# Chunk 0 of a streaming encoder: four engines' queues written in another order

## The chip, the cores and the metric

The kernel runs on one core of one Trainium2 chip. A core has a matrix engine (TensorE, PE in the profile), a vector engine (VectorE, DVE), an activation engine (ScalarE, ACT), a general engine (GpSimd, POOL) and a queue that starts transfers (SyncE, SP). Each executes its own list strictly in order, and they meet only at semaphores. The metric is the device time of one execution in microseconds. Before the change it was 1473.51 us (median of 3 runs, 1473.25 to 1474.21).

## The reference, cut to what matters

One inference step of a one-layer encoder on 4096 prompt rows of 1024 channels, and on 64 sample rows.

```
h = rmsnorm(x) * norm_g
u = h @ w_in                  # 1024 x 2816: eleven splits of 256 columns
a_b, a_c, a_x, a_g, b_v, b_a, b_g, c_u, c_g, x_q, x_g = split(u)
y_a = a_b * conv3(a_c * a_x) * silu(a_g)
y_b = silu(layernorm(conv31(b_v * sigmoid(b_a)))) * silu(b_g)
y_c = (pool_linear(trailing_means(c_u) - c_u)) * pool_scale * silu(c_g)
y_x = softmax(x_q @ mem_k) @ mem_v * silu(x_g)
x = x + concat(y_a, y_b, y_c, y_x) @ w_out ;  y = rmsnorm(x) * final_norm_g
```

`mem_k`, `mem_v` of the prompt are projections of a normed memory of 256 rows. The outputs also hold the convolution and pooling states and the memory keys and values.

## The kernel before, in words

The prompt is worked in 16 chunks of N = 256 rows, and each chunk in two convolution channel tiles (CT = 2). Chunk 0 is written out apart (`first_chunk` on each engine), chunks 1 to 14 are a loop, and chunk 15 is written out with the sample. Chunk 0 does, beside a chunk's own work, all that is done once:

- **The input weights are split into two half precision parts.** 22 tiles of 1024 x 128 arrive by DMA. For tile j ACT squares it (`w_square(j)`, line 1123), PE sums the squares over partitions (`weight_sums(g)`, lines 640 and 642, one for two tiles), DVE makes a power of two from the sum (`w_scale(g)`, lines 1570 to 1575), ACT writes the high part (`w_high(j)`, line 1130) and DVE the low part (`w_low(j)`, line 1584). A projection of PE (`project`, lines 621 to 623, 48 matmuls of 256 columns) takes tiles 2g and 2g+1 of its split; the splits are in the order b_a, b_v, x_q, c_u, a_c, a_x, a_b, a_g, b_g, c_g, x_g, so b_g takes tiles 16 and 17, c_g 18 and 19, x_g 20 and 21.
- **The output weights are split into 16 pieces and stored.** SP loads piece p (`load_piece`, line 405), ACT writes its high part (`piece_hi`, line 1116), POOL its low part (`piece_lo`, line 2097), SP stores both parts (`keep`, line 409). The staging buffer has 4 slots, the ring 8.
- **The prompt memory** is projected in eight `memory_product` steps (line 875), and keys and values are split.
- **The sample** is normed, transposed on PE (`sample_transposes`, line 693), split by ACT (`sample_hi`) and DVE (`sample_lo`), and its eleven projections of 64 columns (`sample_project(g)`, lines 621 to 623 with `hs`, 48 matmuls each) fill PSUM banks that ACT copies out (`raw_keep(0)` after groups 0 to 3, `raw_keep(1)` after 4 to 7, line 1081).

The convolution of width 31 is 31 steps of two instructions on DVE (`taps(0, N, k0, k1)` does steps k0 to k1 - 1, line 1603). The attention is done for two pairs of heads: `scores(p)` on PE, `softmax_max(p)` and `softmax_rcp(p)` on DVE, `exps(p)` (line 1159) and `probs_hi(p)` (line 1173) on ACT, `probs_lo(p)` on DVE (lines 1630 and 360), then a transposition through memory on SP (`probs_leave(p)`, line 473, and `probs_arrive(p)`, line 477), then `attend(p)` on PE (line 730).

Three banks of PSUM (`U`) take the projections of chunk 0 in turn. The list `FIRST` says in which order, and `emptied` makes an entry wait until the entry three places before it has been read (`EMPTIED`): `b_g` waits for the third place before it, and so on. The bank of `a_b` is free when DVE has done `ab_out` (line 1726), that of `w9` when DVE has done `w_scale(9)`.

```
if type(i) is int and i == 0:
    n = FIRST.index(name) - 3
...
"a_b": (conv_a, 4 * CT), "a_g": (ag_ok, 1),
"mix": (mix_ok, 1), "b_g": (bg_ok, 1), "zf": (zt_ok, 1), "c_g": (cg_ok, 1),
```

After the projections PE runs the 16 output pieces (`out_pieces`), with `attend(0, N, 1)`, three sample groups and the transposes of z between them. Then chunk 1 begins.

Of the kernel before, what the change touches and what calls it, by code (L numbers as in the profile page):

```python
# [35 lines left out]
N = 256  # L36
# [20 lines left out]


FIRST = ["w0", "w1", "w2", "b_a", "b_v", "w3", "x_q", "w4", "w5", "w6", "c_u", "w7", "w8", "a_c", "a_x",
         "w9", "a_b", "a_g", "b_g", "w10", "c_g", "mix", "x_g", "zf", "zb", "r0", "r1", "r2", "r3"]  # L60


SAMPLE_SLOTS = {"mix": (1, 2), "zf": (2, 0), "zb": (3, 0)}
# [6 lines left out]
RAW, RING = 4, 8  # L70
Y_ORDER = [0, 4, 6, 2]
PIECES = 2 * KT
# [22 lines left out]
def encoder_program(nc, x_prompt, x_sample, mem_prompt, state_conv_a, state_conv_b, state_pool,  # L95
# [5 lines left out]
    with ctx:  # L101
# [292 lines left out]
        def _(sp):  # L394
# [50 lines left out]
            sp.wait_ge(kv_ok.sem, 2)  # L445
            for dst, off in ((new_k, 0), (new_v, GW)):
                sp.dma_start(dst[0, 0].rearrange("(t p) h d -> p t (h d)", p=P), kv[:, :, off:off + GW]).then_inc(kv_in.sem, 16)
            for p in range(RAW, PIECES):
                keep(p - RAW)
                load_piece(p)  # L450


            def store_states(k, outs):
                sp.wait_ge(st_ok.sem, 2 * k + 2)
# [31 lines left out]
            def probs_leave(i, p, n):  # L486
                sp.wait_ge(p_t_ok.sem, p_t_ok.at(i, p + 1))
                last = type(i) is int and i == CHUNKS
                put_out(probs_turned[PAIRS if last else p], work(i).turned_p, min(n, P), probs_out[p])
# [21 lines left out]
                sp.dma_start(ring[:, q % RING].bitcast(F32), wo_split[q]).then_inc(wo_in[q % RING].sem, 16)  # L511

            def first_sync(x_here, y_here, x_next, x_after):
                probs_leave(0, 0, N)
                for p in range(PIECES - RAW, PIECES):
                    keep(p)
                probs_arrive(0, 0, N)
                raw_leaves(0)
                probs_across(0, 1, N)
                sp.dma_start(xp, x_next).then_inc(x_in[1].sem, 16)  # L520
                raw_leaves(1)
                sp.wait_ge(wlo_ok.sem, FT)
# [96 lines left out]
        def _(pe):  # L619
# [259 lines left out]
            def first_chunk():  # L879
                pe.wait_ge(ident_ok.sem, 2)  # L880
                transposes(0, ob[:, 0])
                pe.wait_ge(tiny_ok.sem, 1)
                weight_sums(0)
                transposes(1, ob[:, 1])
                constants()
                weight_sums(1)
                weight_sums(2)
                project(0, N, "b_a")
                project(0, N, "b_v")
                memory_transposes(0, ob[:, 0])  # L890
                memory_transposes(1, ob[:, 1])
                weight_sums(3)
                project(0, N, "x_q")
                memory_product(0)
                weight_sums(4)
                for k in range(1, 4):
                    memory_product(k)
                weight_sums(5)
                memory_product(4)
                weight_sums(6)  # L900
                sample_transposes()
                memory_product(5)
                project(0, N, "c_u")
                memory_product(6)
                weight_sums(7)
                weight_sums(8)
                memory_product(7)
                project(0, N, "a_c")
                keys_t(0)
                value_sum(0)  # L910
                project(0, N, "a_x")
                scores(0, N, 0)
                weight_sums(9)
                project(0, N, "a_b")
                project(0, N, "a_g")
                scores(0, N, 1)
                for g in range(4):
                    sample_project(g)
                project(0, N, "b_g")
                weight_sums(10)  # L920
                for g in range(4, 7):
                    sample_project(g)
                project(0, N, "c_g")
                sample_project(7)
                attend(0, N, 0)
                mix(0, N)
# [12 lines left out]
                out_pieces(0, N, PIECES - 2 * CT, PIECES)  # L939
# [95 lines left out]
        def _(act):  # L1035
# [230 lines left out]
            def first_chunk(nxt):  # L1266
# [40 lines left out]
                for k in range(16, 18):  # L1307
                    w_square(k)
                w_high(11)
                sample_hi()  # L1310
                w_square(18)
                cu_out(0, N)
                w_high(12)
                keys_values()
                w_high(13)
# [7 lines left out]
                piece_hi(1)  # L1323
                scaled_out(0, N, "a_c", gate[:, 1, :, 0:N], ACT.Copy, ac_ok)
                w_high(15)
                for k in range(2, 5):
                    piece_hi(k)
                w_high(16)
                piece_hi(5)
                exps(0, N, 0)  # L1330
                for k in range(6, 8):
                    piece_hi(k)
                w_high(17)
                piece_hi(8)
                w_high(18)
                piece_hi(9)
                w_square(20)
                piece_hi(10)
                w_square(21)
                piece_hi(11)  # L1340
                d_high(0, N)
                probs_hi(0, N, 0)
                piece_hi(12)
                w_high(19)
                for k in range(13, 15):
                    piece_hi(k)
                act.wait_ge(wsq_ok.sem, FT)
                scaled_out(0, N, "a_g", gate[:, 2, :, 0:N], ACT.Silu, ag_ok)
                piece_hi(15)
                raw_keep(0)  # L1350
                exps(0, N, 1)
                for k in range(20, 22):
                    w_high(k)
                probs_hi(0, N, 1)
                b_gate(0, N)
                mixed(0, N)
                y_high(0, N, 0, ya[:, :, 0:N], ya_ok)
                c_gate(0, N)
# [102 lines left out]
        def _(dve):  # L1461
# [316 lines left out]
            def first_chunk(nxt):  # L1778
# [38 lines left out]
                sample_rms()  # L1817
                sample_scale()
                taps(0, N, 10, 11)
                pool_weights_lo()  # L1820
                taps(0, N, 11, 13)
                for k in range(9, 11):
                    w_low(k)
                taps(0, N, 13, 14)
                w_scale(6)
                taps(0, N, 14, 15)
                w_low(11)
                sample_lo()
                taps(0, N, 15, 16)
                w_scale(7)  # L1830
                w_low(12)
                taps(0, N, 16, 18)
                for k in range(13, 15):
                    w_low(k)
                taps(0, N, 18, 19)
                taps(0, N, 19, 20)
                keys_lo(0)
                w_scale(8)
                value_scale(0)
                taps(0, N, 20, 21)  # L1840
                values_lo(0)
                va_out(0, N)
                softmax_max(0, N, 0)
                w_low(15)
                taps(0, N, 21, 22)
                pool_diff(0, N)
                w_low(16)
                w_scale(9)
                softmax_rcp(0, N, 0)
                conv_a_taps(0, N)  # L1850
                taps(0, N, 22, 23)
                w_low(17)
                ab_out(0, N)
                probs_lo(0, N, 0)
                softmax_max(0, N, 1)
                w_low(18)
                taps(0, N, 23, 24)
                w_low(19)
                taps(0, N, 24, 25)
                ya_out(0, N)  # L1860
                d_low(0, N)
                w_scale(10)
                softmax_rcp(0, N, 1)
                for k in range(20, 22):
                    w_low(k)
                probs_lo(0, N, 1)
                taps(0, N, 25, 31)
                yx_out(0, N)
                z_stats(0, N)
                z_norm(0, N)  # L1870
# [331 lines left out]
```

## Time and profile before

| | |
|---|---|
| median of 3 runs | 1473.51 us |
| the profiled execution | 1474.04 us, of it the span of instructions 1472.2 us |
| PE busy | 1430.6 us (97% of the span) |
| DVE busy | 1180.9 us (80%) |
| ACT busy | 561.3 us (38%) |
| POOL busy | 216.5 us (15%) |
| mean granted TensorE clock | 0.996 of full |
| stretch of chunk 0 on PE | 0 to 166.1 us |

The times of the profile are those of the profiled execution, 0.5 us above the median of the runs. A matmul's busy time is modelled and overlaps its neighbours, so the distance between two starts is the better measure of what it costs.

### The profile page before, as it was taken

How to read it: one execution, taken by the hardware profiler on the slowest of the kernel's cores; microseconds unless marked ns; L12 is line 12 of the kernel's file. 1: busy time of each engine (PE TensorE's matmuls, PEld its weight loads, DVE VectorE, ACT ScalarE, POOL GpSimd, SP SyncE). 2: the span in 40 equal slices, each digit the busy share in tenths (PEclk: the TensorE clock that was granted, in tenths of full speed). 3: DMA queues.
4: the chain of work that ended last, by engine and by line, in shares of the span. 5: the costliest groups of instructions: out<-in, count | busy, mean ns of one | idle time of the engine just before them, and what ended most of it. 6: DMA issues, size and time to landing. Idle time of an engine off the chain costs nothing.

```text
span 1472.2 us, 32643 instructions
## 1 busy us (share of the span) xinstructions
PE 1430.6 (97%) x11766; PEld 1224.2 (83%) x11766; DVE 1180.9 (80%) x3087; ACT 561.3 (38%) x1237; POOL 216.5 (15%) x180
## 2 busy tenths in 40 slices
PE   5898999999999999999999999999999999999997
PEld 4687888888888888888888888888888888888875
DVE  6896696987959697895959789695968869596897
ACT  7775243333324333332434233243423423242342
POOL 0062011111101111110111111011111111111111
PEclk9999999999999999999999999999999999999999
DMA  9976455555364556446355654635565463545663
GB/s 265 259 268 211 170 174 188 200 199 199 114 239 146 185 199 227 172 128 252 118 197 188 228 185 139 251 107 203 182 215 187 160 247 91 216 168 199 231 206 118
DMA packets 127522, 280.88 MB, mean 191 GB/s; under 512 B 12297, under 2 KB 69309, under 8 KB 127485
## 3 DMA queue, kind: packets, MB, share of 16 engines
q1 hardware_dynamic: 127485, 280.40, 55.3%
q8 instruction: 22, 0.36, 0.1%
q14 instruction: 15, 0.12, 0.0%
HBM read 221.86 MB, written 58.49 MB: 190 GB/s over the span
## 4 chain that ended last, share of the span: by engine, by line
PE 87%; DVE 6%; DMA 2%; issue 2%; ACT 2%; SPq 2%; POOL 0%; ACTq 0%; DVEq 0%
PE u L621 20%; PE u L622 19%; PE u L623 19%; PE sps L621 5%; PE sps L623 4%; PE sps L622 4%; PE qps L621 4%; PE qps L623 4%; PE qps L622 4%; PE ops L730 2%; DVE z L1603 1%; DMA ring<-wo_split 1%; DMA w_hl<-in_w_in 1%; DVE w_hl L1584 1%; SPq L397 1%
## 5 line engine op out<-in xcount | busy, mean ns | idle before, releaser
L621 PE MATMUL u<-h_hi,w_hl 128*128 128x256 f16 x2816 | 770.1, 273 | 2.8 <-DVE w_hl L1584 2.7
L622 PE MATMUL u<-h_lo,w_hl 128*128 128x256 f16 x2816 | 769.1, 273 | 0.0
L623 PE MATMUL u<-h_hi,w_hl 128*128 128x256 f16 x2816 | 769.0, 273 | 0.0
L1603 DVE SCALAR_TENSOR_TENSOR z<-glu,cst,z 128x256 f32<-128x256 f32 x960 | 412.3, 499 | 0.5
L621 PEld LDWEIGHTS u<-h_hi,w_hl 128*128 128x128 f16 x2816 | 276.4, 98 | 47.4 <-issue 7.9
L623 PEld LDWEIGHTS u<-h_hi,w_hl 128*128 128x128 f16 x2816 | 276.1, 98 | 32.5
L622 PEld LDWEIGHTS u<-h_lo,w_hl 128*128 128x128 f16 x2816 | 276.2, 98 | 32.2 <-issue 0.7
L1050 ACT ACTIVATE gate<-u,inv 128x256 f32<-128x256 f32 x192 | 79.5, 466 | 113.8 <-PE u L623 113.5
L2107 POOL TENSOR_TENSOR sa<-cu 128x540 f32<-128x540 f32 x16 | 30.0, 1877 | 548.6 <-ACT cu L1050 477.9
L621 PE MATMUL sps<-ring,y_hi 128*128 128x512 f32 x256 | 101.8, 398 | 2.3 <-POOL y_lo L2092 2.1
L621 PE MATMUL qps<-ring,y_hi 128*128 128x512 f32 x256 | 101.8, 398 | 0.5 <-DMA ring<-wo_split 0.5
L623 PE MATMUL sps<-ring,y_lo 128*128 128x512 f32 x256 | 100.1, 391 | 0.0
L623 PE MATMUL qps<-ring,y_lo 128*128 128x512 f32 x256 | 100.0, 391 | 0.0
L622 PE MATMUL sps<-ring,y_hi 128*128 128x512 f32 x256 | 99.8, 390 | 0.0
L622 PE MATMUL qps<-ring,y_hi 128*128 128x512 f32 x256 | 99.7, 389 | 0.0
L1263 ACT ACTIVATE junk<-ob 128x1024 bf16<-128x1024 f32 x32 | 33.8, 1057 | 171.1 <-DVE ob L2030 170.6
L2092 POOL TENSOR_TENSOR y_lo<-ya,y_hi 128x512 fp32r<-128x512 f32 x16 | 20.7, 1292 | 471.4 <-ACT y_hi L1179 471.4
L2030 DVE TENSOR_TENSOR ob<-sps,ob 128x512 f32<-128x512 f32 x32 | 20.6, 685 | 82.4 <-PE sps L623 82.4
L1159 ACT ACTIVATE probs<-sps,st 128x256 f32<-128x256 f32 x128 | 58.9, 472 | 58.4 <-DVE st L1611 58.4
L1173 ACT ACTIVATE prow<-probs,st 128x256 f16<-128x256 f32 x128 | 59.7, 564 | 56.1 <-DVE st L1621 56.1
L1489 DVE SCALAR_TENSOR_TENSOR st<-st 128x1 f32<-128x1 f32 (+1 forms) x303 | 73.1, 268 | 4.9
L1050 ACT ACTIVATE dq_hi<-u,inv 128x256 fp32r<-128x256 f32 x32 | 13.4, 470 | 129.3 <-PE u L623 129.3
(317 smaller groups left out, 1978.5 us busy)
## 6 DMA issues: line engine op xcount, KB each, us to landing
ring<-wo_split SPq DMA_DIRECT2D x248, 512.0 KB, 7.8
ob<-in_x_prompt SPq DMA_DIRECT2D x34, 512.0 KB, 4.2
probs_turned<-probs SPq DMA_DIRECT2D x128, 128.0 KB, 2.4
pt<-probs_turned SPq DMA_DIRECT2D x32, 512.0 KB, 3.6
out<-ob SPq DMA_DIRECT2D x32, 512.0 KB, 3.1
rows_turned<-rows SPq DMA_DIRECT2D x112, 128.0 KB, 2.4
w_hl<-in_w_in SPq DMA_DIRECT2D x20, 512.0 KB, 7.3
wo_split<-ring SPq DMA_DIRECT2D x16, 512.0 KB, 5.0
```

What stands on the lines that cost most here:

```text
L621: nc.tensor.matmul(out, a_hi, b_hi, start=first, stop=False)
L622: nc.tensor.matmul(out, a_hi, b_lo, start=False, stop=False)
L623: return nc.tensor.matmul(out, a_lo, b_hi, start=False, stop=last)
L730: ins = nc.tensor.matmul(bank[h * HD:(h + 1) * HD, o:o + n].rearrange("d (t i j) -> d t i j", t=nt, j=SQ), v[:, va, k, d:d + HD], pt[:, b, ...
L1050: ins = nc.scalar.activation(dst[:, c], u[:, c, 0:n], func, scale=inv[:, f:f + 1])
L1159: ins = nc.scalar.activation(b.probs[0:m, t, h, :], bank[0:m, h, t * NMEM:(t + 1) * NMEM], ACT.Exp, bias=b.nmax[0:m, s, h:h + 1], scale=1. ...
L1173: ins = nc.scalar.activation(b.prow[0:m, t, h, :, 0], b.probs[0:m, t, h, :], ACT.Copy, scale=b.rcp[0:m, s, h:h + 1])
L1263: nc.scalar.activation(junk[0:m, :], ob[0:m, t, :] if n == N else xs, ACT.Square, accum_out=O_SQ[0:m, t:t + 1]).then_inc(o_sq.sem, 1)
L1489: nc.vector.scalar_tensor_tensor(w[:, e], y[:, e], v[:, e], y[:, e], ALU.mult, ALU.mult).then_inc(s.sem, 1)
L1603: ins = nc.vector.scalar_tensor_tensor(z[:, c, 0:n], glu[:, c, k:k + n], w, z[:, c, 0:n], ALU.mult, ALU.add)
L2092: nc.gpsimd.tensor_tensor(b.y_lo[:, k:k + CT, 0:n], src, b.y_hi[:, k:k + CT, 0:n].bitcast(F32), ALU.subtract).then_inc(y_lo_ok.sem, 1)
L2107: nc.gpsimd.tensor_tensor(sa[:, :, 0:S2 + n], cu[:, :, 1:HP + n], cu[:, :, 0:HP + n - 1], ALU.add).then_inc(win_ok.sem, 1)
```

## The change

Nothing is computed differently, and no instruction is added or taken away. In chunk 0 the lists of PE, ACT, DVE and SP are written in another order, and two neighbours in `FIRST` change places.

- **PE:** `sample_transposes` stands behind `memory_product(5)` and `project c_u` and no longer ahead of them. `weight_sums(10)` and `project b_g` stand ahead of `sample_project(0..3)` and no longer behind them.
- **FIRST:** `w10` ahead of `b_g`. So `b_g` now takes the bank that `a_b` had, `w10` the one that `w9` had; `mix` follows `w10` in its bank and `x_g` follows `b_g`.
- **ACT:** `cu_out` ahead of `sample_hi`; the pieces `piece_hi(2..15)`, the high halves 16 to 21, both `exps` and both `probs_hi` interleaved in another way; `b_gate` far ahead; `raw_keep(0)` behind piece 9 and no longer behind piece 15.
- **DVE:** low halves 9 to 21 ahead of convolution steps that stood ahead of them; steps 18 to 24 go behind.
- **SP:** `probs_leave(0, 0, N)` between `load_piece(11)` and `keep(8)`, and no longer behind `load_piece(15)`.

```diff
 FIRST = ["w0", "w1", "w2", "b_a", "b_v", "w3", "x_q", "w4", "w5", "w6", "c_u", "w7", "w8", "a_c", "a_x",
-         "w9", "a_b", "a_g", "b_g", "w10", "c_g", "mix", "x_g", "zf", "zb", "r0", "r1", "r2", "r3"]
+         "w9", "a_b", "a_g", "w10", "b_g", "c_g", "mix", "x_g", "zf", "zb", "r0", "r1", "r2", "r3"]
@@ SP
-            for p in range(RAW, PIECES):
-                keep(p - RAW)
-                load_piece(p)
...
+                for p in range(RAW, PIECES - RAW):
+                    keep(p - RAW)
+                    load_piece(p)
                 probs_leave(0, 0, N)
+                for p in range(PIECES - RAW, PIECES):
+                    keep(p - RAW)
+                    load_piece(p)
@@ PE
-                sample_transposes()
                 memory_product(5)
                 project(0, N, "c_u")
+                sample_transposes()
                 memory_product(6)
...
                 scores(0, N, 1)
+                weight_sums(10)
+                project(0, N, "b_g")
                 for g in range(4):
                     sample_project(g)
-                project(0, N, "b_g")
-                weight_sums(10)
@@ ACT
+                cu_out(0, N)
                 sample_hi()
                 w_square(18)
-                cu_out(0, N)
...
                 act.wait_ge(wsq_ok.sem, FT)
                 scaled_out(0, N, "a_g", gate[:, 2, :, 0:N], ACT.Silu, ag_ok)
+                piece_hi(9)
+                raw_keep(0)
+                piece_hi(10)
+                b_gate(0, N)
+                piece_hi(11)
+                w_high(20)
+                w_high(21)
+                exps(0, N, 1)
+                piece_hi(12)
+                piece_hi(13)
+                probs_hi(0, N, 1)
+                piece_hi(14)
                 piece_hi(15)
-                raw_keep(0)
-                exps(0, N, 1)
-                for k in range(20, 22):
-                    w_high(k)
-                probs_hi(0, N, 1)
-                b_gate(0, N)
@@ DVE
                 va_out(0, N)
                 softmax_max(0, N, 0)
-                w_low(15)
-                taps(0, N, 21, 22)
+                w_low(16)
+                conv_a_taps(0, N)
+                w_low(17)
+                softmax_rcp(0, N, 0)
                 pool_diff(0, N)
-                w_low(16)
-                w_scale(9)
-                softmax_rcp(0, N, 0)
-                conv_a_taps(0, N)
-                taps(0, N, 22, 23)
-                w_low(17)
                 ab_out(0, N)
+                w_low(18)
                 probs_lo(0, N, 0)
                 softmax_max(0, N, 1)
-                w_low(18)
-                taps(0, N, 23, 24)
                 w_low(19)
-                taps(0, N, 24, 25)
-                ya_out(0, N)
                 d_low(0, N)
                 w_scale(10)
+                w_low(20)
+                w_low(21)
+                ya_out(0, N)
+                taps(0, N, 18, 20)
                 softmax_rcp(0, N, 1)
-                for k in range(20, 22):
-                    w_low(k)
+                taps(0, N, 20, 21)
                 probs_lo(0, N, 1)
-                taps(0, N, 25, 31)
+                taps(0, N, 21, 31)
```

Two places as they stand in the built programs; names in brackets are the semaphores that a row waits for. First PE behind the second scores (`sps<-kt_hi,dq_hi`), before the change: the sample groups are the `qps<-hs,w_hl` rows, b_g the next `u<-h_hi,w_hl`, the weight sum the two `128x2` rows.

```order
L621 MATMUL sps<-kt_hi,dq_hi 128x256 [waits exp_ok]
...
L621 MATMUL qps<-hs,w_hl 128x64 [waits mn_ok,xs_step]
...
L621 MATMUL u<-h_hi,w_hl 128x256 [waits wlo_ok,wscl_ok]
...
L621 MATMUL u<-h_hi,w_hl 128x256 [waits wlo_ok]
...
L640 MATMUL u<-tiny,ones 128x2 [waits conv_a]
L642 MATMUL u<-w_sq,ones 128x2 [waits wsq_ok]
L621 MATMUL qps<-hs,w_hl 128x64
```

And the same place on PE with the change:

```order
L623 MATMUL sps<-kt_hi,dq_hi 128x256 [waits exp_ok]
...
L642 MATMUL u<-tiny,ones 128x2 [waits wscl_ok]
L644 MATMUL u<-w_sq,ones 128x2 [waits wsq_ok]
L623 MATMUL u<-h_hi,w_hl 128x256 [waits wlo_ok,conv_a]
...
L623 MATMUL u<-h_hi,w_hl 128x256 [waits wlo_ok]
...
L623 MATMUL qps<-hs,w_hl 128x64 [waits mn_ok,xs_step]
```

What moved: b_g stands ahead of the first four sample groups, and waits for `conv_a` (`ab_out` on DVE) where it waited for `wscl_ok`.

Then ACT from the copy of the first sample bank (`raw_stage<-qps`, which waits for `raw_ready` of PE) on, before the change; `ring<-rows` is a piece of the output weights, here the last of them, `probs,st<-sps,st` the second exponentials, `w_hl<-ob,w_scl` high halves 20 and 21:

```order
L1116 ACTIVATE ring<-rows 128x512 [waits wo_kept7,raw_in3]
L1081 ACTIVATE raw_stage<-qps 128x512 [waits raw_ready]
L1159 ACT_TABLE_LOAD [waits probs_out0]
L1159 ACTIVATE probs,st<-sps,st 128x256 [waits nmax_ok]
...
L1130 ACTIVATE w_hl<-ob,w_scl 128x1024 [waits wlo_ok,wscl_ok] x2
L1173 ACTIVATE prow<-probs,st 128x256 [waits exp_ok,p_t_ok,rcp_ok]
```

The same place on ACT with the change:

```order
L1083 ACTIVATE raw_stage<-qps 128x512 [waits raw_ready]
L1118 ACTIVATE ring<-rows 128x512 [waits wo_kept2,raw_in2]
L1052 ACTIVATE gate<-u,inv 128x256 [waits u_ready,glu_ok]
...
L1118 ACTIVATE ring<-rows 128x512 [waits wo_kept3,raw_in3]
L1132 ACTIVATE w_hl<-ob,w_scl 128x1024 [waits wlo_ok,wscl_ok] x2
L1161 ACT_TABLE_LOAD [waits probs_out0]
...
L1118 ACTIVATE ring<-rows 128x512 [waits wo_kept4,raw_in0]
L1118 ACTIVATE ring<-rows 128x512 [waits wo_kept5,raw_in1]
L1175 ACTIVATE prow<-probs,st 128x256 [waits exp_ok,p_t_ok,rcp_ok]
...
L1118 ACTIVATE ring<-rows 128x512 [waits wo_kept7,raw_in3]
```

What moved: six pieces of the output weights, the second exponentials and the last two high halves stand behind the copy of the first sample bank.

## Rows read from the trace of the kernel before

**Rows 1.** Stretches of PE: us, busy (x count), granted clock, DMA share, GB/s.

```profile
134.10:166.10 32.00, 30.26 (x280) 1.00 0.55 208
166.10:300.00 133.90, 133.73 (x1139) 1.00 0.49 174
```

**Rows 2.** Waits of PE, 24 to 170 us: us in total, times, longest.

```profile
PE ops L693 <- DVE raw_stage L1512: 4.4, 1, 4.4
...
PE u L621 <- DVE w_hl L1584: 2.7, 3, 1.9
PE u L621 <- ACT gate L1050: 2.2, 2, 2.0
...
PE ops L730 <- DMA pt<-probs_turned: 1.3, 1, 1.3
```

**Rows 3.** Granted clock of three stretches on PE, columns as in rows 1.

```profile
58.70:62.30 3.60, 3.60 (x12) 0.54 1.18 289
...
107.10:109.70 2.60, 2.55 (x24) 1.00 1.03 400
...
127.20:130.60 3.40, 3.40 (x18) 0.51 0.64 154
```

**Rows 4.** Timeline of PE: start, us, operation, [idle before <- releaser].

```profile
96.87 0.20 PE L621 MATMUL qps<-hs,w_hl 128*128 128x64 f16 x1
...
102.48 0.27 PE L621 MATMUL u<-h_hi,w_hl 128*128 128x256 f16 x1
...
123.52 0.90 PE L730 MATMUL ops<-pt,v 128*64 128x256 f16 x12 [1.27 <-DMA pt<-probs_turned]
...
134.10 0.48 PE L621 MATMUL sps<-ring,y_hi 128*128 128x512 f32 x1
...
145.16 0.64 PE L774 MATMUL u<-ident,z 128*128 128x128 f32 x4
```

**Rows 5.** Timeline of DVE, 70 to 134 us.

```profile
70.26 0.16 DVE L1570 TENSOR_SCALAR w_exp<-u 128x2 int32<-128x2 int32 x1 [1.75 <-PE u L642]
...
78.34 2.71 DVE L1603 SCALAR_TENSOR_TENSOR z<-glu,cst,z 128x256 f32<-128x256 f32 x4
...
85.36 0.88 DVE L1692 SCALAR_TENSOR_TENSOR va<-u,inv,gate 128x256 f32<-128x256 f32 x2 [1.53 <-ACT gate L1050]
...
89.25 2.94 DVE L1603 SCALAR_TENSOR_TENSOR z<-glu,cst,z 128x256 f32<-128x256 f32 x2
...
104.00 0.87 DVE L1603 SCALAR_TENSOR_TENSOR z<-glu,cst,z 128x256 f32<-128x256 f32 x2
...
107.01 0.86 DVE L1726 SCALAR_TENSOR_TENSOR ya<-u,inv,ya 128x256 f32<-128x256 f32 x2
...
126.83 6.82 DVE L1603 SCALAR_TENSOR_TENSOR z<-glu,cst,z 128x256 f32<-128x256 f32 x12
```

**Rows 6.** Timeline of POOL: four pieces without a break, and the last.

```profile
86.96 6.38 POOL L2097 TENSOR_TENSOR ring<-rows,ring 128x512 fp32r<-128x512 f32 x4 [0.99 <-ACT ring L1116]
...
115.24 1.29 POOL L2097 TENSOR_TENSOR ring<-rows,ring 128x512 fp32r<-128x512 f32 x1 [1.38 <-ACT ring L1116]
```

**Rows 7.** Timeline of ACT, 112 to 125 us.

```profile
112.51 1.28 ACT L1050 ACT_TABLE_LOAD   x1
...
115.05 0.60 ACT L1081 ACTIVATE raw_stage<-qps 128x512 f32<-128x512 f32 x1
...
117.61 0.47 ACT L1159 ACTIVATE probs<-sps,st 128x256 f32<-128x256 f32 x1
...
120.31 2.19 ACT L1130 ACTIVATE w_hl<-ob,w_scl 128x1024 f16<-128x1024 f32 x2 [0.77 <-DVE w_scl L1573]
122.40 1.84 ACT L1173 ACTIVATE prow<-probs,st 128x256 f16<-128x256 f32 x4
```

**Rows 8.** Timeline of SP's queue (issue times), 114 to 119 us.

```profile
114.42 3.15 SPq L409 DMA_DIRECT2D wo_split<-ring  x4
117.61 1.22 SPq L477 DMA_DIRECT2D pt<-probs_turned  x1
```

More of the change, by code:

```diff
@@ L1325, in first_chunk @@
                 w_high(15)
-                for k in range(2, 5):
-                    piece_hi(k)
                 w_high(16)
-                piece_hi(5)
[L1330 to L1333, printed above, removed]
-                piece_hi(8)
[L1335 to L1346, printed above, removed]
+                piece_hi(2)
+                piece_hi(3)
+                w_high(17)
+                w_square(20)
+                exps(0, N, 0)
+                piece_hi(4)
+                w_square(21)
+                piece_hi(5)
+                w_high(18)
+                piece_hi(6)
+                w_high(19)
+                d_high(0, N)
+                piece_hi(7)
+                probs_hi(0, N, 0)
+                piece_hi(8)
                 act.wait_ge(wsq_ok.sem, FT)
                 scaled_out(0, N, "a_g", gate[:, 2, :, 0:N], ACT.Silu, ag_ok)
-                piece_hi(15)
-                raw_keep(0)
-                exps(0, N, 1)
-                for k in range(20, 22):
-                    w_high(k)
-                probs_hi(0, N, 1)
-                b_gate(0, N)
+                piece_hi(9)
[10 more added lines that the diff above has]
+                piece_hi(14)
+                piece_hi(15)
                 mixed(0, N)
@@ L1819, in first_chunk @@
                 taps(0, N, 10, 11)
+                for k in range(9, 11):
+                    w_low(k)
+                w_scale(6)
                 pool_weights_lo()
                 taps(0, N, 11, 13)
-                for k in range(9, 11):
-                    w_low(k)
+                w_low(11)
                 taps(0, N, 13, 14)
-                w_scale(6)
+                sample_lo()
                 taps(0, N, 14, 15)
-                w_low(11)
-                sample_lo()
-                taps(0, N, 15, 16)
                 w_scale(7)
                 w_low(12)
[L1832 to L1836, printed above, removed]
+                taps(0, N, 15, 16)
+                w_scale(8)
+                w_low(13)
+                taps(0, N, 16, 17)
                 keys_lo(0)
-                w_scale(8)
                 value_scale(0)
-                taps(0, N, 20, 21)
+                w_low(14)
                 values_lo(0)
+                w_low(15)
+                taps(0, N, 17, 18)
+                w_scale(9)
                 va_out(0, N)
                 softmax_max(0, N, 0)
-                w_low(15)
-                taps(0, N, 21, 22)
+                w_low(16)
+                conv_a_taps(0, N)
+                w_low(17)
+                softmax_rcp(0, N, 0)
                 pool_diff(0, N)
-                w_low(16)
-                w_scale(9)
-                softmax_rcp(0, N, 0)
-                conv_a_taps(0, N)
-                taps(0, N, 22, 23)
-                w_low(17)
                 ab_out(0, N)
+                w_low(18)
                 probs_lo(0, N, 0)
                 softmax_max(0, N, 1)
-                w_low(18)
-                taps(0, N, 23, 24)
                 w_low(19)
-                taps(0, N, 24, 25)
-                ya_out(0, N)
                 d_low(0, N)
                 w_scale(10)
+                w_low(20)
+                w_low(21)
+                ya_out(0, N)
+                taps(0, N, 18, 20)
                 softmax_rcp(0, N, 1)
-                for k in range(20, 22):
-                    w_low(k)
+                taps(0, N, 20, 21)
                 probs_lo(0, N, 1)
-                taps(0, N, 25, 31)
+                taps(0, N, 21, 31)
                 yx_out(0, N)
```

## The prediction

> **What bounds the kernel now.** I read the busy shares first, then stretches of PE, then the waits of PE, then the timelines of DVE, ACT, POOL and SP in chunk 0. From 166.1 us on PE is the bound: 133.73 of 133.90 us busy in the stretch shown, at the full clock [rows 1]. Nothing there is moved, so a shift of the point where chunk 1 starts (166.1 us) is a shift of the whole, and I price that point alone. In chunk 0 PE waits: 4.4 us for the scaled sample rows, 2.7 for low halves, 2.2 for banks that ACT empties, 1.3 for the turned probabilities [rows 2]. Two of these waits also cost clock: behind the 4.4 us one the granted clock is 0.54 for 3.6 us, and in 127.2 to 130.6, behind two waits, 0.51 for 3.4 us; behind the 1.9 us wait it stays at 1.00 [rows 3]. These are the levels of 1.2 and 2.4 GHz.
>
> **The change part by part.**
>
> *Sample transposes behind c_u.* `memory_product(5)` and c_u need nothing that is late at 54.3 us, so the 4.4 us go [rows 2], and with them the low clock: 3.6 x 0.46 = 1.7 us [rows 3]. Together 6.0 us; I take back 0.3 since a_b and a_g now reach their banks earlier than ACT and DVE free them. PE ends the second scores at 96.9 - 5.8 = 91.1 us, where it stood at 96.87 [rows 4]. Bounds 90.5 and 92.5.
>
> *b_g ahead of the first sample groups.* Before, PE did groups 0 to 3 here, 102.48 - 96.87 = 5.6 us [rows 4], without a wait. Now the weight sum takes 0.4, and at 91.5 us b_g wants the bank of a_b, so `ab_out`. That ended at 107.01 + 0.86 = 107.9 us [rows 5]. How early can it be? Steps 18 to 22 of the convolution leave DVE's list ahead of it, ten instructions: four at 78.34 (2.6 us), two like those at 104.00 (0.8), two at 89.25 (2.9), two at 104.00 (0.8), together 7.1 us [rows 5]. DVE's waits of 1.75 and 1.53 us [rows 5] end, since the weight sum and a_c come earlier: 3.3. A new one comes, for high half 15, which stands on ACT behind the reading of a_c: 2.2, by laying out ACT's list from a_c on. And fewer pieces disturb DVE. A pair of steps took 2.94 us beside POOL's four pieces and 0.87 us without [rows 5, 6], so a piece costs DVE about (2.94 - 0.87) / 2 = 1.0 us; by 97 us some three pieces fewer have run than had by 107: 3.1. So `ab_out` ends at 107.9 - 7.1 - 3.3 + 2.2 - 3.1 = 96.6 us. Bounds: 94.4 without the new wait, 99.7 if as many pieces fall in it. The Trainium skill, SBUF — State Buffer, "Who interferes with whom", says the port pair that VectorE and GpSimd share is an exclusive lock for a whole instruction; the trace agrees (1.47 us for a step of 0.43), and by a halved bandwidth instead of a lock a step would have lost only about 0.4 us and `ab_out` would come at 98.4.
>
> So PE, whose sample groups are ready but stand behind b_g, idles from 91.5 to 96.6: 5.1 us. The 4.4 us wait was followed by the half clock for 3.6 us [rows 2, 3], and this one is longer, so b_g costs 5.2 + 1.7 = 6.9 us and ends at 103.5; with 5.6 for the groups, `raw_ready` comes at 109.1 where it came at 102.5. If the clock holds, 1.7 less. The Trainium skill, TensorE: Matmul & The Clock Gate, "What's actually happening", has throttled as the default and activity as what releases it; the trace agrees (0.54 behind 4.4 us), and by its rule both new waits below cost clock, while without it the sum would be 1.7 us smaller.
>
> *What is queued behind that.* ACT meets `raw_keep(0)` after piece 9 at about 101 us. Before, it stood behind piece 15 and found its bank full (it ran at 115.05 [rows 7], released at 102.5). Now ACT stands still some 8 us, to 109.1, and behind it in its list are pieces 10 to 15, b_gate, high halves 20 and 21, the second exponentials. Their time: the copy and six pieces 7 x 0.53 = 3.7 (a piece is as large as the copy, 0.60 less the overlap with the next), b_gate 0.7, halves 2.1, table load 1.3, four exponentials 4 x 0.46 = 1.8, probs_hi 1.8, and an estimated 0.8 of waiting for DVE's reciprocal, which now stands behind four convolution instructions: 12.2 us [rows 7]. Piece 15 is done by ACT at 121.3; it was done 0.2 us before POOL took it at 115.24 [rows 6].
>
> *SP.* POOL takes pieces 14 and 15 back to back, to 123.5. `probs_arrive(0)` still stands behind `keep(15)`, as before, when SP issued the four last keeps at 114.42 and the arrival at 117.61 [rows 8], 1.1 us behind the end of POOL's last piece. Moving `probs_leave(0)` ahead buys nothing here, since the arrival is the later half. With one keep to issue behind POOL (3.15 / 4 = 0.8) it is now issued at 124.2. The data released PE at 123.52 [rows 4], 5.9 us after issue, behind a burst of four keeps; now the keeps are spread, and I take 5.0 (bounds 4.4 and 5.9). PE attends at 129.2 instead of 123.52.
>
> *What PE has until then.* Groups 4 to 6 (4.2 us), c_g (5.2, its low halves are now early, so the wait of 0.6 to 0.8 there ends), group 7 (1.4): 109.1 + 10.8 = 119.9. So it idles 9.3 us where it idled 1.3, and no later work is there to fill it.
>
> *To the output pieces.* From the attention to the first piece it was 134.10 - 123.52 = 10.6 us [rows 4]. Of it 2.0 was the wait of `mix` for b_g's bank [rows 2], which goes: `mix` now follows w10. The low clock there stays (it comes earlier). 10.6 - 2.0 = 8.6, less 0.1: the pieces start at 137.7 instead of 134.1.
>
> *Behind that.* DVE has 20 convolution instructions after the last turn of the probabilities, not 12 at 6.82 us [rows 5]: 11.4 us from 125.5, some waiting included, to 134.6 to 137. The transposes of z need them 11 us behind the first piece (145.16 - 134.10 [rows 4]), at 148.7. So they are hidden; uncovered, they would cost up to 4.5 us. The tail keeps its 32.0 us [rows 1].
>
> **The sum.** Chunk 1 starts at 137.7 + 32.0 = 169.7 instead of 166.1: +3.6 us. I take 0.2 off for small waits that end with earlier low halves: +3.4. The profiled execution would be 1474.04 + 3.4 = 1477.4 us, and the median, 0.5 below it, 1473.51 + 3.4 = **1476.9 us**.
>
> **The rivals.** What a measurement of this kernel can tell from no change is about 0.2%, 2.9 us.
>
> 1. *Same mechanism, but it cancels.* The order costs PE 5.1 + 9.3 us of idle time and gives back 4.4 + 1.7 + 2.7 + 2.0 of waits and clock. If the clock holds behind the first new wait (-1.7) or the arrival takes 4.4 us (-0.6), the sum is +1.1 to +2.8. For it: a wait of 1.9 us cost no clock [rows 3]. Against it: 5.1 is more than 4.4. Time 1475.4.
> 2. *Faster: `ab_out` decides, and comes early.* Place: b_g's bank. If DVE is done with `ab_out` by 94.4 and the clock holds, b_g ends at 99.6, `raw_ready` is at 105.2, everything behind it 3.9 us earlier, and with the arrival's lower bound (-0.6) the attention at 124.7. At the full clock (-1.6) the pieces start at 131.6, 2.5 us early, with the small waits 2.7. With `ab_out` at 93.0 it is -4.1. It decides from about 94 us. For it: ten instructions and two waits leave DVE's list. Against it: the steps that leave are short ones, and the low halves that stay each waited behind a piece. Time 1470.1.
> 3. *The order does all it seems to aim at.* b_g starts at once, ACT never stands, all waits of rows 2 but the last end: 4.4 + 1.7 + 2.7 + 2.2 = 11 us, time 1462.5. Against it: `conv_a` would have to be there at 91.5, 16 us earlier than it was.
> 4. *Worse than the sum.* `ab_out` at 99.7, arrival at 5.9 us: +3.1 + 0.9 on the sum, 1480.9.
>
> **How the numbers follow.** Forecast 0.46, rival 1 0.27, rival 2 0.14, rival 3 0.04, rival 4 0.09. Half a us on each of the three large terms spreads the forecast over 1475.5 to 1478.8, so about 0.10 of its 0.46 lies within 2.9 us of before. Slower by over 0.2%: 0.36 + 0.09 = 0.45. Within 0.2%: 0.10 + 0.27 = 0.37. Faster: 0.14 + 0.04 = 0.18. The likeliest case's own range is 1475.5 to 1478.8. The range that should hold it 8 times in 10 reaches into rivals 2 and 4: 1470.5 to 1480.0.
>
> **What would show each step.** In the profile of the changed kernel: the 4.4 us wait before the sample transposes gone, and the memory product behind it at full clock; a PE wait of about 5 us before b_g, released by DVE's `ab_out`; a clock near 0.5 behind it; ACT idle about 8 us before the copy of the first sample bank, released by PE; piece 15 at about 121 us; a PE wait of about 9 us for the turned probabilities; no wait before `mix`; the last convolution step before 140 us; PE solid behind 170 us. I am wrong if b_g waits under 2 us, or if ACT does not stand at that copy, or if the attention starts before 126 us.

## The result and the profile after

The changed kernel takes 1479.5 us (median of 7 runs, 1477.15 to 1480.67) and the kernel before 1473.59 us (7 runs beside it, 1472.71 to 1476.45). The ratio is 1.0034, 95% interval 1.0024 to 1.0044: slower, by about 5 us. The profiled execution took 1477.46 us, of it 1475.7 the span.

The stretches of PE, columns us, busy (x count) of PE, PEld, DVE, ACT and POOL, granted clock, DMA share, GB/s:

```profile
91.90:97.10 5.20, 0.58 (x7) 0.50 (x5) 5.09 (x9) 2.35 (x4) 3.08 (x3) 0.97 0.77 259
97.10:103.90 6.80, 6.80 (x50) 5.51 (x51) 6.68 (x7) 5.07 (x10) 4.85 (x3) 0.77 0.75 269
103.90:109.60 5.70, 5.70 (x199) 5.70 (x197) 2.55 (x6) 0.00 (x0) 0.00 (x0) 1.00 0.86 228
128.80:138.20 9.40, 9.40 (x67) 7.75 (x67) 5.00 (x13) 4.15 (x7) 2.62 (x2) 0.70 0.61 205
...
138.15:170.14 31.99, 30.24 (x279) 25.01 (x277) 13.73 (x48) 7.35 (x14) 4.16 (x3) 1.00 0.51 185
```

Chunk 1 starts at 170.14 us (166.08 before) and the tail in front of it is 31.99 us as before [rows 1]: the loss, 4.1 us at this point, lies ahead of the output pieces. Clock is lost over b_g (0.77) and from the attention to the pieces (0.70). These are mixtures of the levels 1.2 and 2.4 GHz.

The waits of PE, 24 to 175 us (us in total, times, longest), against [rows 2]:

```profile
PE ops L732 <- DMA pt<-probs_turned: 7.1, 1, 7.1
PE u L623 <- DVE ya L1729: 4.6, 1, 4.6
...
PE qps L625 <- issue: 1.0, 1, 1.0
PE u L623 <- DVE va L1695: 0.9, 1, 0.9
```

The wait for the sample rows (4.4), those for low halves (2.7) and that of `mix` (2.0) are gone; two new ones of 11.7 us together stand in their place. The timeline of PE, against [rows 4]:

```profile
54.31 1.96 PE L877 MATMUL sps<-probs,mem_rows 128*128 128x512 f32 x4
...
97.09 0.40 PE L623 MATMUL u<-h_hi,w_hl 128*128 128x256 f16 x1 [4.62 <-DVE ya L1729]
...
114.85 0.27 PE L623 MATMUL u<-h_hi,w_hl 128*128 128x256 f16 x1
...
128.78 1.49 PE L732 MATMUL ops<-pt,v 128*64 128x256 f16 x12 [7.13 <-DMA pt<-probs_turned]
...
138.15 0.47 PE L623 MATMUL sps<-ring,y_hi 128*128 128x512 f32 x1
```

The four queues behind b_g's wait, in the order of the chain. DVE [rows 5], then ACT [rows 7], POOL [rows 6] and SP's issues [rows 8]:

```profile
80.35 1.28 DVE L1587 SCALAR_TENSOR_TENSOR w_hl<-w_hl,w_scl 128x1024 f16<-128x1024 f32 x1 [2.25 <-issue]
...
96.16 0.88 DVE L1729 SCALAR_TENSOR_TENSOR ya<-u,inv,ya 128x256 f32<-128x256 f32 x2
...
125.83 7.97 DVE L1606 SCALAR_TENSOR_TENSOR z<-glu,cst,z 128x256 f32<-128x256 f32 x20
```

```profile
109.66 0.60 ACT L1083 ACTIVATE raw_stage<-qps 128x512 f32<-128x512 f32 x1 [7.46 <-PE qps L625]
...
111.90 2.19 ACT L1132 ACTIVATE w_hl<-ob,w_scl 128x1024 f16<-128x1024 f32 x2
...
119.97 1.13 ACT L1118 ACTIVATE ring<-rows 128x512 fp32r<-128x512 f32 x2
```

```profile
119.18 4.36 POOL L2096 TENSOR_TENSOR ring<-rows,ring 128x512 fp32r<-128x512 f32 x3
```

```profile
120.69 3.20 SPq L409 DMA_DIRECT2D wo_split<-ring  x3
123.93 0.46 SPq L473 DMA_DIRECT2D pt<-probs_turned  x1
```

Read downward it is one chain: `ab_out` ends at 97.0, b_g and group 3 end at 109.5, ACT stood 7.46 us for them, pieces 14 and 15 end at 121.1, POOL's low parts at 123.5, the arrival is issued at 123.9, PE attends at 128.8. Of the work that stands behind the copy `raw_keep(0)` on ACT, only the six pieces and their place among the rest are new: the second exponentials, high halves 20 and 21 and `b_gate` stood behind it before too.

### The profile page after: what moved, and what is told of

Its sections match the earlier page's. It is cut to its first block, busy times and chain, and to the rows that moved or that the text cites. A ratio compares the mean times of both kernels' runs of the same rounds, so it can differ in the third digit from the quotient of the medians.

```text
span 1475.7 us, 32643 instructions
## 1 busy us (share of the span) xinstructions
PE 1430.9 (97%) x11766; PEld 1225.2 (83%) x11766; DVE 1177.3 (80%) x3087; ACT 560.4 (38%) x1237; POOL 217.5 (15%) x180
## 4 chain that ended last, share of the span: by engine, by line
PE 88%; DVE 5%; issue 2%; SPq 2%; ACT 1%; DMA 1%; POOL 1%; ACTq 0%; DVEq 0%; POOLq 0%
PE u L623 20%; PE u L624 19%; PE u L625 19%; PE sps L623 5%; PE qps L623 4%; PE sps L625 4%; PE sps L624 4%; PE qps L625 4%; PE qps L624 4%; PE ops L732 2%; DVE z L1606 1%; DMA w_hl<-in_w_in 1%; DVE w_hl L1587 1%; SPq L397 1%; PE u L788 0%
```

## Experiments

All runs in one table, each described below. Where an edit isn't named as standing on another, it is made to the changed kernel, "c_u first alone" to the kernel before. "raw_keep(0)" is its start on ACT, "piece 15" is the end of its high part on ACT, "attend" the start of PE's first attention, "chunk 1" the first matmul of chunk 1, all from the profiled execution; the ratio is that of the runs to before, with its interval. It compares with runs of the kernel before on the same chip. Three chips were used: the first four experiments ran on one (before: 1473.59 us), the bank, "c_u and DVE" and "gate early" on a second (1473.17), the last two on a third (1474.89). So the ratios tell which kernel is faster, and the profiled times only where in an execution time went.

| kernel | raw_keep(0) | piece 15 | arrival issued | attend | chunk 1 | profiled us | ratio |
|---|---|---|---|---|---|---|---|
| before | 115.05 | 115.2 | 117.61 | 123.52 | 166.08 | 1474.04 | 1 |
| changed | 109.66 | 121.1 | 123.93 | 128.78 | 170.14 | 1477.46 | 1.0034 (1.0024 to 1.0044) |
| b_g put back | 102.41 | 118.7 | 120.60 | 125.22 | 166.72 | 1474.07 | 0.9997 (0.9988 to 1.0006) |
| raw_keep late | 116.69 | 116.8 | 118.72 | 125.11 | 165.54 | 1473.49 | 1.0001 (0.9992 to 1.0010) |
| b_g's bank | 102.58 | 118.2 | 120.18 | 125.11 | 165.38 | 1472.65 | 1.0012 (1.0003 to 1.0021) |
| arrival ahead | 110.96 | 122.4 | 122.36 | 127.16 | 168.87 | 1476.14 | 1.0010 (1.0001 to 1.0019) |
| c_u first alone | 112.34 | 112.5 | 114.94 | 122.97 | 164.19 | 1472.48 | 0.9981 (0.9971 to 0.9991) |
| c_u and DVE | 110.20 | 110.3 | 112.17 | 118.49 | 166.38 | 1473.68 | 1.0011 (1.0002 to 1.0019) |
| gate early | 110.17 | 110.3 | 111.41 | 118.03 | 156.91 | 1465.27 | 0.9949 (0.9937 to 0.9961) |
| changed, again | 109.86 | 121.3 | 124.08 | 129.80 | 170.87 | 1478.66 | 1.0028 (1.0016 to 1.0039) |
| b_g put back, SyncE as before | 102.57 | 122.9 | 125.68 | 130.47 | 171.26 | 1479.11 | 1.0030 (1.0018 to 1.0041) |

### b_g put back

The order on PE and, with it, the order of the banks are those of before.

```diff
-         "w9", "a_b", "a_g", "w10", "b_g", "c_g", "mix", ...
+         "w9", "a_b", "a_g", "b_g", "w10", "c_g", "mix", ...
...
-                weight_sums(10)
-                project(0, N, "b_g")
                 for g in range(4):
                     sample_project(g)
+                project(0, N, "b_g")
+                weight_sums(10)
```

> The changed kernel with TensorE's order of this place undone alone: b_g and the last weight sum again behind the sample's groups 0 to 3, in the banks of before (b_g in w9's bank, w10 in a_b's). ScalarE, VectorE, GpSimd and SyncE as changed. The theory (b_g's wait for a_b's bank makes group 3 late, ScalarE stands at raw_keep(0) with pieces 10 to 15 behind it, and piece 15 holds the arrival of the first probabilities): group 3 ends about 97.5 instead of 109.5, raw_keep(0) does not wait, ScalarE stands at b_gate until b_g is done (about 103), piece 15 is done about 115 to 116 instead of 121, attend(0) starts about 123.3 instead of 128.8, chunk 1 starts about 164.7 instead of 170.1, and the time is 5 us under the changed kernel: 0 to 2 us under before. Rival A (the order of ScalarE itself, pieces thinned out between high halves and exponentials, makes them late): attend(0) stays at 128 to 129 and the time at that of the changed kernel, 0.3% over before. Rival B (only the 4.6 us wait and the low clock of TensorE cost): TensorE reaches attend(0) earlier and waits there for as much longer, time as changed.

Measured: the 5 us are gone, as the theory says, and attend comes 3.6 us earlier. It comes 1.9 us later than expected: piece 15 is done at 118.7, since ACT waits 2.99 us for `w_scale(10)` and 1.14 us for piece 15's row. PE arrives earlier and waits longer:

```profile
125.22 1.49 PE L732 MATMUL ops<-pt,v 128*64 128x256 f16 x12 [10.46 <-DMA pt<-probs_turned]
```

So PE's wait of 4.6 us was not the price by itself; the late arrival was. That b_g acted on it through ACT is what the next run tests, and whether it was b_g's place or its bank, the one after.

### raw_keep late

```diff
-                raw_keep(0)
                 piece_hi(10)
...
                 piece_hi(15)
+                raw_keep(0)
                 mixed(0, N)
```

> The changed kernel with one ScalarE instruction moved: raw_keep(0) behind piece 15 instead of ahead of piece 10. TensorE's order, its 4.6 us wait at b_g and the low clock behind it stay. The theory: ScalarE then stands only until b_g is done (103.9), some 5.6 us less, piece 15 is done about 115 to 116, attend(0) starts about 123 to 123.5 and the time is 5 us under the changed kernel, though TensorE waits at b_g as before. Rival B (TensorE's wait at b_g and its low clock are the loss): the time stays at that of the changed kernel, 0.3% over before. Rival A (ScalarE's order apart from raw_keep): no change either, attend(0) at 128 to 129.

Measured: one ACT instruction moved gives the whole loss back, with b_g's wait still there and the clock at 0.57 from 96 to 103 us. Waits of PE, then of ACT at b_g's gate:

```profile
PE u L623 <- DVE ya L1729: 3.9, 1, 3.9
...
PE ops L732 <- DMA pt<-probs_turned: 3.4, 1, 3.4
```

```profile
104.56 0.84 ACT L1052 ACTIVATE gate<-u,inv 128x256 f32<-128x256 f32 x2 [2.74 <-PE u L625]
```

This rules out the rival that PE's wait at b_g is itself the loss. Attend was expected at 123 to 123.5 and came at 125.11: pieces 13 and 15 wait 0.26 and 1.15 us for their rows, and the arrival needs 6.4 us from its issue to attend.

### b_g's bank

```diff
-         "w9", "a_b", "a_g", "w10", "b_g", "c_g", "mix", ...
+         "w9", "a_b", "a_g", "b_g", "w10", "c_g", "mix", ...
...
-                weight_sums(10)
                 project(0, N, "b_g")
+                weight_sums(10)
```

> The changed kernel with the two neighbours b_g and w10 in the other order alone, in the table of banks and on TensorE: b_g again takes w9's bank, w10 a_b's, and b_g still runs ahead of the sample's groups. If the wait for a_b's bank is what made b_g's early place dear (the theory): b_g starts at 92 to 92.5 without a wait and runs at the full clock (5.3 us instead of 6.8), w10 stands after it behind ab_out (97.0), so it waits under 0.5 us, groups 0 to 3 end about 103 to 103.5, ScalarE waits at raw_keep(0) 1 to 2 us instead of 7.5, attend(0) starts about 123.5 to 125.3 as with b_g put back (125.2 there), and the time is 4.5 to 6 us under the changed kernel, within 0.1% of before. If b_g's place ahead of the groups itself is the cost, whatever its bank: group 3 is late by b_g's length, attend(0) is at 127 or later and the time at least 0.2% over before.

Measured: b_g starts at 91.2 without a wait, its stretch (91.2 to 97.3) is at clock 1.00, and PE then waits 11.69 us for the probabilities instead of 7.13. Attend is as expected (125.11). By the ratios 3.2 us come back (1.0034 to 1.0012), less than the 4.5 to 6 expected, while the profiled execution gives 4.8. So most of the cost came with the bank and not with b_g's place ahead of the groups. Whether the place costs something too is not settled: by the ratios this kernel is 2.2 us slower than b_g put back (1.0012 against 0.9997), and in the profiled executions its chunk 1 starts 1.3 us earlier.

### The arrival ahead of two keeps

```diff
-                for p in range(PIECES - RAW, PIECES):
+                for p in range(PIECES - RAW, PIECES - 2):
                     keep(p)
                 probs_arrive(0, 0, N)
+                for p in range(PIECES - 2, PIECES):
+                    keep(p)
```

> The changed kernel with one SyncE instruction moved: the arrival of the first pair's probabilities ahead of the keeping of pieces 14 and 15, behind that of 13. The theory (GpSimd's low parts of pieces 12 to 15, 1.4 us apart, are the last link ahead of the arrival): attend(0) starts 3 to 4 us earlier (about 125.2 instead of 128.8), its wait falls from 7.1 to about 3.5 us, and the time falls by 3 to 3.7 us to within 0.1% of before's, if nothing later takes it back. Rival C (the probabilities' own way through DRAM or the queue is last): attend(0) moves by less than 1 us and the time stays 0.3% over before. Rival D (the second pair or the sample's groups 8 to 10 are late next): attend(0) early, but the pieces 4 to 8 wait and chunk 1 starts at 169 to 170.

Measured: 3.5 us by the ratios (1.0034 to 1.0010), as the theory says. In the profile attend moves by 1.6 only, since in that execution group 3 ended 1.3 us later than in the changed kernel's (raw_keep(0) at 110.96; b_g's stretch from 97 to 110 us had clock 0.78 against 0.88). So the keeps of the last two pieces, which wait for POOL's low parts, are the last link ahead of the arrival. The length of the low clock behind b_g's wait is not the same in each execution.

### c_u first alone

```diff
-                sample_transposes()
                 memory_product(5)
                 project(0, N, "c_u")
+                sample_transposes()
...
+                cu_out(0, N)
                 sample_hi()
                 w_square(18)
-                cu_out(0, N)
```

> The kernel before with one part of the change alone: c_u ahead of the sample's transposes on TensorE, and its eviction ahead of the sample's high part on ScalarE. If the 4.4 us wait at the transposes is worth its length by itself, chunk 1 starts 5 to 6 us earlier than in before (160.5 instead of 166.1), the time is 0.35 to 0.4% under before. The theory: the gain needs VectorE's new order, since low halves 14 to 17 stand there behind taps as before and TensorE catches up with them: b_g's and c_g's starts are within 2 us of before's (102.5 and 115.1), small waits appear at a_b and at the scores, and the time is 0 to 2 us under before (ratio 0.9985 to 1.0).

Measured: 2.8 us faster than before, between the two readings, and c_g starts at 112.0, 3.1 us early where the second reading had under 2. Of the 5.8 us that PE wins at the transposes, chunk 1 keeps 1.9 in the profile. Part goes in small waits for gates and low halves (1.03, 0.86, 0.73 and 1.58 us on the timeline), and the last part in a transfer. The issues from 111 to 123 us, with the median us to landing, of this kernel:

```profile
wo_split<-ring SPq DMA_DIRECT2D x4, 512.0 KB, 4.4
pt<-probs_turned SPq DMA_DIRECT2D x1, 512.0 KB, 7.9
```

and of the changed kernel from 119 to 129 us:

```profile
pt<-probs_turned SPq DMA_DIRECT2D x1, 512.0 KB, 4.7
```

The same arrival takes 7.9 us here and 4.7 there, and PE waits 4.17 us for it. Here four keeps of 512 KB were issued in 3.5 us ahead of it, there in 4.6. The spacing alone doesn't explain it: the arrival took 5.8 us in the kernel before (four keeps in 3.15 us) and 6.3 us with raw_keep late (four keeps in 5.4 us). No run changed the spacing alone, so the cause of the longer transfer stays open.

### c_u and VectorE's order

ACT, SP and b_g's place as in the run before this one, VectorE's list as in the changed kernel.

> Before with two parts of the change: c_u ahead of the sample's transposes (as in the run with that part alone) and VectorE's whole new order. ScalarE's pieces, SyncE's order and b_g's place are those of before. It differs from the run with b_g put back by ScalarE's and SyncE's orders only (and w_high's places that go with them). Theory now: those two orders hold back the arrival by their thinned pieces and late loads; without them piece 15 is done at 106 to 109 (118.7 there, 114.5 before), attend(0) starts at 117 to 119.5 (125.2 there, 123.0 with c_u alone); then mix is next and waits 3 to 5 us for b_g's gate on ScalarE, which stands there behind the second exponentials and the last high halves. So the time comes out about that of c_u alone (1469 to 1473), 0 to 0.3% under before. The other reading (VectorE's taps put off, z and the gates are late next): mix and attend early, but the pieces behind z_rows wait for z, chunk 1 no earlier than before, time 1473 to 1476.

Measured: attend as expected (118.49), piece 15 a little later (110.3, expected 106 to 109). But the time is no better than before: with c_u first alone the ratio was 0.9981, and VectorE's new order on top makes it 1.0011, 4.4 us more. With this order of ACT, VectorE's new order costs time, although attend comes 4.5 us earlier. `mix` waits, 5.7 us where 3 to 5 were expected, and behind the wait the stretch of 9.3 us to the pieces has clock 0.70:

```profile
118.49 0.89 PE L730 MATMUL ops<-pt,v 128*64 128x256 f16 x12 [1.43 <-DMA pt<-probs_turned]
...
125.08 0.58 PE L621 MATMUL u<-dq_hi,pw_hi 128*128 128x256 f32 x1 [5.70 <-ACT gate L1050]
```

The expectation had added up the wait and left out its clock; it also missed that the second reciprocal stands behind late low halves on VectorE, so that ACT waits 4.04 us ahead of `probs_hi(1)` and its gate behind it. My expected 1469 to 1473 was wrong by 2 us; the ratio's interval begins at 1.0002.

### Gate early

```diff
                 raw_keep(0)
+                b_gate(0, N)
+                for k in range(20, 22):
+                    w_high(k)
                 exps(0, N, 1)
-                for k in range(20, 22):
-                    w_high(k)
                 probs_hi(0, N, 1)
-                b_gate(0, N)
```

On top of the run before, with the arrival ahead of `keep(14)` and `keep(15)` as above.

> As the run before (c_u first, VectorE's new order), and three single moves: on ScalarE b_g's gate right behind raw_keep(0) (ahead of the second exponentials) and high halves 20 and 21 ahead of those exponentials, on SyncE the arrival of the first probabilities ahead of the keeping of pieces 14 and 15. Theory: every wait that the runs so far showed between 92 and 130 us is then met: attend(0) starts at 116.5 to 118.5, mix behind it waits under 1 us, z_rows starts 5 to 8 us earlier than in before (145.2), and the time is 1466 to 1469, 0.3 to 0.5% under before. If a transfer takes it back (1.5 MB of kept pieces around 110 to 116 us delays the arrival, or the out pieces' reloads), z_rows moves by 3 us or less and the time is 1470 to 1472; if VectorE's late taps end last, z_rows waits for z and the time is that of before.

Measured: 1465.47 us (6 runs, 1465.04 to 1468.69), 0.51% under before, and the fastest of the kernels here. It is a little more than expected: the transposes of z start at 136.0, 9 us earlier than before, where 5 to 8 were expected. PE has no wait at attend or `mix`, and from 92 to 130.9 us the clock stays at 1.00 (columns as in the first fence of this text):

```profile
118.03 0.85 PE L732 MATMUL ops<-pt,v 128*64 128x256 f16 x12
...
124.80 0.48 PE L623 MATMUL sps<-ring,y_hi 128*128 128x512 f32 x1
```

```profile
92.00:118.00 26.00, 24.70 (x511) 22.97 (x508) 24.65 (x33) 21.48 (x38) 14.57 (x10) 1.00 0.94 333
118.00:130.90 12.90, 12.66 (x94) 10.33 (x90) 12.48 (x24) 7.32 (x14) 4.00 (x3) 1.00 0.53 161
```

From attend to the pieces takes 6.8 us here and 9.4 in the changed kernel, with the same instructions. Which of the three moves carries how much was not tried apart.

### The changed kernel again

> The changed kernel once more, unaltered, for a second profile: its seven runs lie between 1477.2 and 1480.7 us with the profiled one among the fastest. If the low clock behind b_g's wait is not of one length from run to run (the run with the arrival moved already had group 3's end at 110.5 instead of 109.1 with the same start of b_g), the second profile has b_g's start within 0.3 us of 97.1, group 3's end anywhere from 109 to 112, ScalarE's raw_keep(0) and everything behind it later by the same, and its time minus that of the first profile is that difference to within 0.5 us. If the spread comes from elsewhere (later chunks), the start of chunk 1 is within 0.3 us of the first profile's whatever the time.

Measured: slower than before again, 1.0028. Of the two readings neither holds whole. b_g starts at 97.12 and raw_keep(0) at 109.86, 0.2 us later than in the first profile. Attend is 1.0 us later (5.7 us from issue to attend, 4.85 in the first), chunk 1 0.7, the time 1.2. So TensorE's clock behind b_g explains little of this pair, the arrival's transfer most of what is lost ahead of chunk 1, and 0.5 us lies behind it. The two profiles are from different rounds, and the kernel before was at 1474.89 us beside the second and at 1473.59 beside the first, so a part of the 1.2 us can be a difference of the chips.

### SyncE's order of before

On top of b_g put back; the order that results is that of before on SP.

```diff
-                for p in range(RAW, PIECES - RAW):
+                for p in range(RAW, PIECES):
                     keep(p - RAW)
                     load_piece(p)
                 probs_leave(0, 0, N)
-                for p in range(PIECES - RAW, PIECES):
-                    keep(p - RAW)
-                    load_piece(p)
```

> The run with b_g put back, with SyncE's order of before on top: the first probabilities leave behind the loads of all sixteen pieces, not ahead of the last four. ScalarE's and VectorE's orders stay as changed. If SyncE's new order is what holds the last pieces back (they are loaded from 105.9 on behind the leaving, ScalarE waits 1.1 us for piece 15's row): pieces 12 to 15 come 1 us earlier and attend(0) starts at 123 to 124.5 instead of 125.2, time 1 us less or the same. If the new order of SyncE helps (the second exponentials wait for the leaving to land, since they write over the same rows): the leaving goes out at 105 to 108 instead of 103.5, the exponentials and pieces 12 to 15 start 2 to 4 us later, attend(0) at 127 to 129, and the time is 0.1 to 0.3% over before.

Measured, beside b_g put back: the second reading, and more of it than expected (attend at 130.47, expected 127 to 129). The leaving is issued at 108.49 instead of 103.53, the second exponentials wait for it, and all behind them is 5 us later:

```profile
115.91 1.28 ACT L1159 ACT_TABLE_LOAD   x1 [5.32 <-DMA probs_turned<-probs]
```

## Why the prediction was right, and where its steps were off

The direction and the mechanism held: slower, by b_g's wait, ACT's stand at `raw_keep(0)` and the late arrival. The profiled execution moved by 3.4 us, which is the forecast sum, but that is in part luck: the start of chunk 1 moved by 4.1 us, where 3.6 was forecast, and 0.6 us came back behind it, where the prediction has nothing. The median moved by 5.9 and the ratio says 5.0.

- **Transposes behind c_u.** Forecast: scores end at 91.1. Measured: near 91.9, 5.0 us earlier than before [rows 4] and not 5.8. Most of the missing 0.8 is the wait for `va_out` at a_g's bank: 0.9, where the sum takes back 0.3.
- **b_g.** `ab_out` forecast to end at 96.6, measured 97.0; wait 5.1, measured 4.62; b_g's own 6.9, measured 6.77. The new DVE wait was forecast at 2.2 and is 2.25. The term for POOL's pieces (3.1 us) fits only as a product: up to `ab_out` POOL took 12 pieces before and 7 in the changed kernel, so five fewer and not three. With the forecast's other terms, 2.7 us are left for it, some 0.5 us a piece and not 1.0 (an estimate from these sums). No run tests the price. The clock rose again before b_g was through: 6.8 us at 0.77 are 1.6 us lost (forecast 1.7). Rival 1, in which it holds, did not happen.
- **ACT's stand.** Forecast some 8 us to 109.1, measured 7.46 to 109.66. Piece 15 forecast at 121.3, measured 121.1: the copy came 0.6 us later than forecast and the 0.8 us of waiting for the reciprocal did not happen, so two errors cancel. The moved `raw_keep(0)` shows that this stand is the cause: without it the ratio is 1.0001.
- **SP.** Arrival forecast at 124.2, measured 123.93; issue to attend forecast at 5.0, measured 4.85 and 5.7. The bound of 5.9 was too low: in the runs where PE waits for it, it was 4.6 to 8.0. The reason given for 5.0, that the keeps are spread, is not shown (see c_u first alone). One sentence of this step misses a path: "Moving `probs_leave(0)` ahead buys nothing here". It weighed the arrival alone; the second exponentials write where the leaving reads, and on the kernel with b_g put back its old place costs 5.3 us of attend. On the changed kernel itself this was not run.
- **PE until then.** Forecast idle 9.3, measured 7.1 and 1.0. c_g started at 114.85, not 113.3. This cost nothing, as PE waited in any case.
- **To the pieces.** Forecast 8.5 us, measured 9.4. The sum carried over the low clock of before. Here 9.4 us at clock 0.70 lose 2.8, where [rows 3] lost 1.7 in 3.4 us. The Trainium skill, TensorE: Matmul & The Clock Gate, "What's actually happening", has idling bring the throttle and activity release it; the trace agrees: 0.70 behind 7.1 us of wait, 1.00 behind none.
- **Behind that.** The 20 late convolution instructions take 7.97 us, where 11.4 was forecast. They end at 133.8 (forecast 134.6 to 137) and are hidden; the tail is 31.99.

The term that missed is the step from the profile to the median. I took the median of before off the profile of before (0.5 us) and kept that for after. The changed kernel's runs spread over 3.5 us and its first profile was among its fastest: 1477.46 against 1478.66 in the second. Executions with long waits of PE differ in how long the clock stays low behind them and in how long the arrival travels; both are seen above (0.78 and 0.88, 4.85 and 5.7 us). Where the remaining 2 us lie, and whether it is in these two at all, stays open.

What gain was possible also came out: the places are in series on one chain (ACT's pieces, POOL, the keeps, the arrival, attend, `mix`). Any one of three edits (b_g put back with its bank, its bank alone, `raw_keep(0)` late) gives back 3 to 5.5 us by the ratios and leaves PE waiting at attend, by up to 11.7 us. The version in which all places are met (gate early) is worth 12.5 us against the changed kernel (1.0034 to 0.9949).

## What to carry to other kernels

Work moved ahead on one engine is worth what the next meeting point leaves of it: trace the chain to the instruction that the engine waits for last, and look on each engine of it for what stands behind a wait that isn't its own. A copy that nobody is waiting for should not stand in a queue ahead of work that is waited for. When banks rotate by a list, changing two neighbours changes whom each waits for; look at that before the order itself.

## What the runs showed of the hardware

- A wait of 7.1 us costs PE 2.6 us more behind it: the same stretch from attention to output pieces takes 9.4 us at clock 0.70 and 6.8 at 1.00. A longer wait does not cost more: behind waits of 3.4, 4.4, 10.5, 11.7 and 16.0 us the stretch took 8.4, 9.7, 9.5, 8.3 and 8.8 us. A wait of 3.0 us (gate early, at 88.2 us) left the clock at 1.00.
- The same transfer of 512 KB landed 4.5 us (b_g put back) to 7.9 us (c_u first alone) after its issue. In both runs four others of 512 KB were issued just ahead, in 5.0 and 3.5 us; why it took longer is open.
- With b_g starting at 97.1 to 97.3, the stretch from 97 to 110 us had a clock of 0.88, 0.86 and 0.78 in three executions of kernels whose lists are equal up to there (changed, changed again, arrival ahead).
